# Modulation vectors of a two-block transformer step: sixteen of their pieces move from TensorE to VectorE, the others are gathered four to a bank

## The reference, cut to what matters

```python
c_act = jax.nn.silu(c)
for i in range(DEPTH):                          # DEPTH = 2
    mod = c_act @ w_mod[i] + b_mod[i]           # 1024 @ 1024 x 6144
    sh1, sc1, g1, sh2, sc2, g2 = jnp.split(mod, 6, axis=-1)
    h = modulate(rmsnorm(x, norm_mix[i]), sh1, sc1)     # h * (1 + sc1) + sh1
    y = pool_mixer(h, ...) if i == 0 else moba_attention(h, w_qkv, w_o, rel_bias)
    x = x + g1[:, None, :] * y
    h = modulate(rmsnorm(x, norm_mlp[i]), sh2, sc2)
    x = x + g2[:, None, :] * squared_relu_mlp(h, w_up[i], w_down[i])
return rmsnorm(x, norm_final)
```

## Time and profile before

| | us |
|---|---|
| median of 3 runs | 1115.1 (1113.09 to 1115.51) |
| the profiled execution's own time | 1114.1 |
| its span, first to last instruction | 1112.3 |
| TensorE busy | 1059.4 (95%) |
| VectorE busy | 771.5 (69%) |
| ScalarE busy | 534.8 (48%) |
| mean granted TensorE clock | 0.990 of full speed |

### The profile page before, as it was taken

One profiled execution on the slowest core, in us unless ns is written; L12 is line 12 of the kernel. 1 busy time (PEld: TensorE's weight loads), 2 busy tenths in 40 slices (PEclk: granted clock), 3 DMA queues, 4 the chain that ended last, 5 costly groups with the idle time before them and its releaser, 6 DMA issues.

```text
span 1112.3 us, 21636 instructions
## 1 busy us (share of the span) xinstructions
PE 1059.4 (95%) x8322; PEld 978.7 (88%) x8322; DVE 771.5 (69%) x1415; ACT 534.8 (48%) x862; POOL 1.7 (0%) x14
## 2 busy tenths in 40 slices
PE   5989999999999989999999999999989999999995
PEld 2469999999888868999999989989878999999995
DVE  5377767444556656877655589899897778777654
ACT  3345655433445545676544534538414565444341
POOL 0000000000000000000000000000000000000000
PEclk9999999999999999999999999999999999999998
DMA  9986666666646565455545435345443555555531
GB/s 360 369 336 252 249 245 229 242 247 226 210 174 218 180 242 227 156 185 189 189 174 204 151 114 200 141 152 209 136 147 119 222 190 183 181 182 183 205 126 38
DMA packets 35791, 222.10 MB, mean 200 GB/s; under 512 B 3804, under 2 KB 9101, under 8 KB 9357
## 3 DMA queue, kind: packets, MB, share of 16 engines
q1 hardware_dynamic: 35724, 221.18, 54.9%
HBM read 220.10 MB, written 1.07 MB: 199 GB/s over the span
## 4 chain that ended last, share of the span: by engine, by line
PE 83%; DVE 10%; ACT 3%; DMA 2%; issue 1%; SPq 0%; DVEq 0%; ACTq 0%
PE bank L534 23%; PE bank L535 22%; PE bank L536 22%; PE bank L785 6%; PE bank L556 4%; PE bank L835 3%; DVE y L1539 2%; PE bank L572 2%; DMA raw<-weights 2%; DVE w_lo L1230 1%; DVE rt L1602 1%; DVE newt L1236 0%; PE bank L705 0%; PE bank L579 0%; DMA x<-x_in 0%
## 5 line engine op out<-in xcount | busy, mean ns | idle before, releaser
L1230 DVE TENSOR_TENSOR w_lo<-raw,w_hi 128x1024 fp32r<-128x1024 f32 x270 | 327.8, 1218 | 65.4 <-ACT w_hi L896 64.3
L534 PE MATMUL bank<-xg_hi,w_hi 128*128 128x258 f32 (+1 forms) x1264 | 362.6, 287 | 5.8 <-DVE w_lo L1230 2.1
L535 PE MATMUL bank<-xg_lo,w_hi 128*128 128x258 f32 (+1 forms) x1264 | 357.9, 283 | 0.0
L536 PE MATMUL bank<-xg_hi,w_lo 128*128 128x258 f32 (+1 forms) x1264 | 357.6, 283 | 0.0
L896 ACT ACTIVATE w_hi<-raw 128x1024 fp32r<-128x1024 f32 x270 | 282.2, 1050 | 107.2 <-PE bank L536 91.1
L534 PEld LDWEIGHTS bank<-xg_hi,w_hi 128*128 128x128 f32 x1264 | 240.5, 190 | 14.0 <-issue 8.8
L535 PEld LDWEIGHTS bank<-xg_lo,w_hi 128*128 128x128 f32 x1264 | 240.0, 190 | 0.2
L536 PEld LDWEIGHTS bank<-xg_hi,w_lo 128*128 128x128 f32 x1264 | 239.8, 190 | 0.0
L534 PE MATMUL bank<-hid_hi,w_hi 128*128 128x256 f32 x512 | 144.7, 283 | 1.7 <-DVE ab L1359 1.7
L535 PE MATMUL bank<-hid_lo,w_hi 128*128 128x256 f32 x512 | 142.9, 279 | 0.0
L536 PE MATMUL bank<-hid_hi,w_lo 128*128 128x256 f32 x512 | 142.8, 279 | 0.0
(11 more groups left out here) (210 smaller groups left out, 1393.9 us busy)
## 6 DMA issues: line engine op xcount, KB each, us to landing
raw<-weights SPq DMA_DIRECT2D x157, 1024.0 KB, 4.8
mod_raw<-w_mod SPq DMA_DIRECT2D x48, 1024.0 KB, 6.2
toep<-bias_by_distance SPq DMA_DIRECT2D x8, 256.0 KB, 5.4
x<-x_in SPq DMA_DIRECT2D x1, 1024.0 KB, 5.0
toep<-bias_by_distance SPq DMA_DIRECT2D x8, 128.0 KB, 4.0
y_out<-yout SPq DMA_DIRECT2D x8, 128.0 KB, 1.8
invc<-inv_count SPq DMA_DIRECT2D x1, 512.0 KB, 13.0
vec<-vectors SPq DMA_DIRECT2D x1, 294.0 KB, 5.2
```

The lines of the kernel that those rows point to most:

```text
L534: pe.matmul(dst, hi, r_hi, start=start, stop=False, skip_group_check=True)
L535: pe.matmul(dst, hi, r_lo, start=False, stop=False, skip_group_check=True)
L536: return pe.matmul(dst, lo, r_hi, start=False, stop=stop, skip_group_check=True)
L1230: ve.tensor_tensor(w_lo[:, at % HL, :], raw[:, slot, (at % 2) * UT * P:(at % 2 + 1) * UT * P], w_hi[:, at % HL, :].bitcast(F32), ALU.subtr ...
```

## The change

The 48 pieces fall into two kinds, and the order in which they come is now a list, `PIECES`.

- **32 pieces stay on TensorE, in eight groups of four.** `cz` is 64 columns wide with the vector in column 31. `rows` of piece r of a group takes the columns from 31-r to 63-r, so that its result lands in row r of each column group, and all four pieces of a group accumulate in one bank. There is one `mod_copy` and one `cols` for a group; the moving operand of `cols` is `pick`, a 128x4 table that VectorE makes once from `ident`. Groups 0 to 4 are the twenty pieces before up0. Group 5 runs behind unit 12 of up0 and its `cols` behind unit 14; groups 6 and 7 run in qkv behind units 6 and 18, their `cols` behind units 10 and 22.
- **16 pieces go to VectorE.** They lie in memory with 128 features on the partitions and the 1024 inputs along the row. `dots` issues two `tensor_tensor_reduce` for each, 128x1024 float32, that multiply with `c_all` (the activated `c` on all partitions), add up, start from the bias, and write one column of `modv`. Twelve of them run in down0, at units 0, 1 and 4 of each eight, four in down1, at unit 0 of each eight.
- SyncE's queue loads all pieces into four slots, at places given by `PIECES_AFTER`. One more transfer spreads `c` over the partitions, and ScalarE applies Silu to it at unit 16 of up0.
- The gains of layer 1 are made from two features' chunks at a time in down0. `shift` for qkv is made at unit 30 instead of 24.
- Loops with a register as counter are written out in up0 and down0 and in half of up1 on all engines, and in down1 on VectorE. `cz` and `c_all` make the tiles larger by 5 KB per partition, and `pick` takes 16 bytes per partition ahead of `rstd`.

```diff
+ROWS = 4
+MOD_BASE = [8 * t for t in (SC1, SH1, G1, SC2, SH2)] + [48 + 8 * t for t in (G1, SC2, SH2)]
+MOD_AT = {("up0", 12): 5, ("qkv", 6): 6, ("qkv", 18): 7}
+COLS_AT = {("up0", 14): 5, ("qkv", 10): 6, ("qkv", 22): 7}
+DOTS = [(base, p) for p in range(4) for base in (8 * G2, 48 + 8 * SC1, 48 + 8 * SH1)] + [(48 + 8 * G2, p) for p in range(4)]
+DOTS_AT = {("down0", 8 * p + at): 3 * p + n for p in range(4) for n, at in enumerate((0, 1, 4))}
+DOTS_AT.update({("down1", 8 * p): 12 + p for p in range(4)})
+PIECES = [("rows", q) for q in range(24)] + [("dots", d) for d in range(12)] + [("rows", 24 + q) for q in range(8)]\
+    + [("dots", 12 + d) for d in range(4)]
+PIECES_AFTER = [2, 3, 4, 5, 13, 14, 15, 16, 23, 24, 25, 27, 28, 29, 31, 32, 33, 35, 36, 37, 41, 42, 43, 44, 48, 49, 50, 51]
...
             def piece(q, s):
 
-                if not isinstance(q, int) or q >= 4:
-                    sp.wait_ge(mod_rows, q - (3 if isinstance(q, int) and q < MOD_FIRST else 1))
-                sp.dma_start(mod_raw[:, s, :], w_mod[one(q)].rearrange("a p n -> p (a n)")).then_inc(mod_in[s], 16)
+                kind, n = PIECES[q]
+                if q >= 4:
+                    before, m = PIECES[q - 4]
+                    if before == "rows":
+                        sp.wait_ge(mod_rows, m + 1)
+                    else:
+                        sp.wait_ge(mod_dots, 2 * m + 2)
+                src = w_mod if kind == "rows" else w_dots
+                sp.dma_start(mod_raw[:, s, :], src[one(n)].rearrange("a p n -> p (a n)")).then_inc(mod_in[s], 16)
...
+            def pair_and_pieces(p):
+                pair(p, p % RAW)
+                if p == 6:
+                    sp.dma_start(c_all[:], bass.AP(c_row.tensor, 0, [[0, P], [1, D]])).then_inc(c_row_in, 16)
+                for q in pieces_after(p):
+                    piece(q, q % 4)
...
+            def rows(q):
+
+                g, r, n = q // ROWS, q % ROWS, ROWS_PIECE[q]
+                pe.wait_ge(mod_in[n % 4], 16 * (n // 4 + 1))
+                if r == 0 and g == 1:
+                    pe.wait_ge(var_done, 1)
+                if r == 0 and g >= 2:
+                    pe.wait_ge(mod_copied, g - 1 if q < MOD_FIRST else g)
+                row_bank = row_banks[g % 2 if q < MOD_FIRST else 0]
                 for k in range(DC):
-                    mm = pe.matmul(row_bank[32 * g:32 * g + 32, 0:SEQ], cz[:, k, :], mod_raw[:, s, SEQ * k:SEQ * (k + 1)],
-                                   start=k < 4, stop=k >= 4, tile_position=(0, 32 * g))
+                    c = k % 4
+                    mm = pe.matmul(row_bank[32 * c:32 * c + 32, 0:SEQ], cz[:, k, 31 - r:63 - r],
+                                   mod_raw[:, n % 4, SEQ * k:SEQ * (k + 1)], start=r == 0 and k < 4, stop=r == ROWS - 1 and k >= 4,
+                                   tile_position=(0, 32 * c), skip_group_check=True)
                 mm.then_inc(mod_rows, 1)
...
             for q in range(MOD_POOL):
-                rows(q, q % 4, mod_landed(q))
+                rows(q)
                 if q == 3:
                     pe.wait_ge(small_in, 48)
                     pe.matmul(banks[0][0:HEADS, 0:384], rbx[:], bkt[:], start=True, stop=True).then_inc(bias_mm, 1)
-                if q:
-                    cols(q - 1, (q - 1) % 2)
+                    pe.wait_ge(pick_done, 1)
+                if q % ROWS == 0 and q:
+                    cols(q // ROWS - 1)
...
+            def dots(d):
+
+                (base, p), n = DOTS[d], DOTS_PIECE[d]
+                if d == 0:
+                    ve.wait_ge(c_row_act, 1)
+                ve.wait_ge(mod_in[n % 4], 16 * (n // 4 + 1))
+                at = base + 2 * p
+                for half in range(2):
+                    w = mod_raw[:, n % 4, half * D:(half + 1) * D]
+                    ve.tensor_tensor_reduce(w, w, c_all[:], 1.0, col("b_mod", at + half), ALU.mult, ALU.add,
+                                            accum_out=modv[:, at + half:at + half + 1]).then_inc(mod_dots, 1)
+                ve.wait_ge(mod_dots, 2 * d + 2)
...
             def down(name, n, i, j, gate, gains):
+                mod_work(name, 8 * i + j)
                 if j % 4 < 3:
                     split(name, i, j)
```

More of the change, by code:

```diff
@@ L451, in _ @@
             for q in range(12, MOD_FIRST):
-                piece(q, mod_slot(q))
-            def mlp_loads(i):
-                for s in range(4):
-                    pair(4 * i + 1 + s, (1 + s) % RAW)
-                    if s >= 2:
-                        piece(2 * i + MOD_FIRST + s - 2, s - 2)
-            mlp_loads(0)
-            with sp.Fori(1, 8) as i:
-                mlp_loads(i)
+                piece(q, q % 4)
+            def pair_and_pieces(p):
[3 more added lines that the diff above has]
+                for q in pieces_after(p):
+                    piece(q, q % 4)
+            for p in range(1, U0["qkv"] // 2):
+                pair_and_pieces(p)
             def toeplitz(a):
@@ L484, in _ @@
                         toeplitz(a)
-                for q in range(DC):
-                    if n == max(1, (3 * q - 2) // 2 + 1):
-                        piece(36 + q, q % 2)
-            for a in range(4):
-                pair(p0 + 12 + a, (p0 + 12 + a) % RAW)
-                piece(44 + a, a % 2)
-            p0 += 16
+            for a in range(8):
+                pair_and_pieces(p0 + 12 + a)
+            p0 += 20
             loops = (U0["glu"] // 2 - p0) // RAW
@@ L571, in cols, with mod_work @@
                 for half in range(2):
-                    mm = pe.matmul(dst[:, at + half:at + half + 1], mod_row[:, s, half * P:(half + 1) * P],
-                                   ones[:, 0:1], start=True, stop=True)
+                    mm = pe.matmul(dst[:, ROWS * half:ROWS * half + ROWS], mod_row[:, g % 2, half * P:(half + 1) * P],
+                                   pick[:], start=True, stop=True)
                 mm.then_inc(mod_cols, 1)
+            def mod_work(name, v):
+                if (name, v) in MOD_AT:
+                    for r in range(ROWS):
+                        rows(ROWS * MOD_AT[name, v] + r)
+                if (name, v) in COLS_AT:
+                    cols(COLS_AT[name, v])
@@ L626, in whole @@
                 mm.then_inc(pe_units, 1)
-            def with_piece(i, j, base):
-                if j % 4 == 2:
-                    rows(2 * i + (MOD_FIRST + base + j // 4), j // 4, 16 * i + (landed_base(j // 4) + 16 + 16 * (base // 2)))
-                if j % 4 == 3:
-                    cols(2 * i + (MOD_FIRST + base + j // 4), j // 4)
-            def landed_base(s):
-                return 16 * sum(mod_slot(q) == s for q in range(MOD_FIRST))
             def down(name, i, j):
@@ L761, in _ @@
                             values(a)
-                        if j <= DC:
-                            cols(36 + j, j % 2)
+                        if j < DC:
+                            mod_work("qkv", v)
                         if j == DC:
@@ L924, in _ @@
             root(1)
-            for q in range(8):
-                mod_copy(q, q % 2)
+            for g in range(2):
+                mod_copy(g)
             act.wait_ge(xr_done, 1)
@@ L999, in down @@
                 if name == "down0":
-                    mod_piece(i, j, 8)
+                    mod_work(name, 8 * i + j)
                 split(name, i, j)
             up_phase("up0", 2)
-            act.wait_ge(gain_done, 3)
-            loop_units(act, "down0", lambda i, j: down("down0", i, j, 1, gain_at(2)))
+            for v in range(32):
+                down("down0", v // 8, v % 8, 1, gain_at(2))
             def exps(a, e):
@@ L1495, in _ @@
                     finish("o", 2, 0, j - 1, lambda m: gain[:, 3, one(m)])
-                if j % 2 == 1 and j < 6:
-                    mod_two(45 + j // 2)
             finish("o", 2, 0, 7, lambda m: gain[:, 3, one(m)])
             up_phase("up1", 4)
-            ve.wait_ge(mod_read, 33)
             clear(3, two=True)
-            loop_units(ve, "down1", lambda i, j: down("down1", 3, i, j, 48 + 8 * G2, lambda m: gain1[:, one(m)]))
+            for v in range(32):
+                down("down1", 3, v // 8, v % 8, 48 + 8 * G2, lambda m: gain1[:, one(m)])
             def scaled(name, v, w=SEQ):
```

230 lines of the change are left out of this document (112 added, 118 removed).

## The result

The changed kernel takes 1079.3 us, the median of four runs (1078.8 to 1081.1), against 1114.5 us for the kernel before on the same chip (four runs): a ratio of 0.969, interval 0.967 to 0.970. The forecast was 1081, in a range from 1072 to 1096. The profiled execution took 1079.2 us, of which 1077.3 are its span.

The account below looks back on a forecast made before the run. TensorE, busy for 95% of the span with 83% of the chain, was taken as the bound. 1114.1 - 5.5 (beginning) - 8.6 (up0) - 12.9 (down0) - 8.5 (qkv, o) + 2.0 (clock) = 1080.6; forecast 1081 us, range 1072 to 1096.

Parts of the forecast that it names:

- VectorE keeps ahead in down0: down0: VectorE's new instructions, 1.3 us each, stay hidden under TensorE's products up to 1.57 us each; 12.9 us gained.
- The first rival: down0: VectorE becomes the bound at 2.26 us per instruction, 14 us lost, 1095 us; chance 0.15.
- the prediction's 1.1: down0: at 1.3 us per instruction, the split for unit 12 of each eight is ready 1.1 us early.
- What a piece costs TensorE: From up0 on: one piece costs TensorE about 1.63 us, priced from stages that differ only in pieces.
- qkv and o: qkv and o: twelve pieces go, two groups come, 10.6 us; 8.5 us taken as arriving, bounds 5 and 10.6.
- a piece in the shadow of the slow transfers: qkv and o: one removed piece lies where TensorE idles behind late weight transfers, so 1.6 us is not gained.
- the last piece of group 7: qkv: this piece is loaded behind `toeplitz` and a pair, wanted some 9 us after; 0.5 us allowed as loss.
- The second rival: Beginning and attention: transfers and attention's own chain hold savings to 1 of 5.5 and 5 of 8.5 us; 1089 us; chance 0.13.
- The beginning: Before up0: `cols` of group 1 starts at 36 instead of 39.88 us; 5.5 us gained in all, bounds 1 and 8.
- The wait for `pick`: Beginning: TensorE's wait for this table, done by 23 us, is hidden by the transfers and costs nothing.
- The clock behind a group: Behind groups of four: the clock falls to half level after one of three groups, costing 2 us; bounds 0 and 6.
- The rest: Remaining stages: down1's new work is hidden, nothing gained or lost; 1 us left in the range for moved tiles.

Follow-up runs that it names:

- (3): The changed kernel with both VectorE reducing instructions of each of the 16 pieces on 8 instead of 1024 columns, transfers kept: 1078.9 us.
- (4): The changed kernel with one more 1024-column multiplication with sum on VectorE for each of down0's 12 pieces, result unused: 1086.0 us.
- (7): The changed kernel with the last two bias-table transfers, `toeplitz(6)` and `toeplitz(7)`, each issued one weight pair later in the queue: 1072.3 us.
- (6): The changed kernel with `cols` of groups 1 to 3 right behind its own group, not behind the next group's first `rows`: 1073.3 us.
- (8): Against the kernel before, gathering only: all 48 pieces stay on TensorE in twelve groups of four, none on VectorE: 1095.3 us, ratio 0.983.
- (11): The changed kernel with 24 tiny memsets added on VectorE before down1: 1077.1 us, a single execution.
- (10): The changed kernel with the edits of (6) and (7) together, and `pick` as spare columns of the `vec` tile: 1068.8 us.

## Why the prediction was right, step by step

**VectorE keeps ahead in down0: right.** The instruction takes 1.27 us and 0.08 for its sum, 1.3 forecast; the step between residuals is 11.31 us; and (3) shows that leaving out the arithmetic gives nothing. The first rival (2.26 us for each) is ruled out by the L1290 row. That the bound lay near is shown by (4): 6.3 us lost, where 14.7 us of the same work were added, because one split in each eight came 1.6 us late. The margin of that split in the changed kernel, 1.2 us, is the prediction's 1.1.

**What a piece costs TensorE: right.** down0 gave back 12.83 us, 12.9 forecast, and up0 8.73, 8.6 forecast. The price of 1.63 us came from twin stages, and it counts what busy time of the group doesn't.

**qkv and o: the mechanism right, the size too small.** 10.47 us came, 8.5 were forecast, 10.6 was the bound. TensorE's busy time fell by 146.02 - 134.92 = 11.1 us, which is 12 x 1.63 less two groups at 4.24. Idle time rose by 0.6. I had taken 1.6 us off for a piece in the shadow of the slow transfers and 0.5 for the last piece of group 7, 2.1 in all, and 0.1 came off the 10.6. The parts were not as I had them: the last piece of group 7 cost 1.60 us of waiting, not 0.5, while a wait of 1.66 us before a `cols` (at 301.5 us before) went with the single pieces. That the sum of idle time hardly changed is in part luck. The second rival named a real thing in the wrong form. The queue behind `toeplitz` is worth 7 us in the changed kernel; the change did not win them, and (7) does. The earlier trace rows show the same kind of wait in the kernel before, but no run took it away there.

**The beginning: the mechanism right, 0.9 us too much.** `cols` of group 1 came at 36.5 us, 36 forecast. The stretch from the pool stage to up0 gave 0.9 us where I had 1. Ahead of it 3.6 us came where I had counted 4.5: `cols` was half a microsecond later than I put it, and the copy inside the eight chunks of `h_pad` gave 0.3 us where 0.5 or so was counted. What I did not see is that the order of `cols` held back more than the change gave: (6) wins another 4.6 us up to up0 with one line moved. The wait for `pick` appears in the trace as 4.6 us of TensorE's time. Transfers keep running at 422 GB/s through it (20 to 24 us), and in (6), where the same wait is 4.7 us long, the chain goes past it along transfers. That speaks for a hidden wait, as forecast; no run took the wait away alone.

**The clock behind a group: wrong.** 2.0 us were counted and nothing came, in any of the three groups, nor in the seven of (8). The reasoning went from the beginning of the kernel before, where single `rows` and `cols` never brought the clock up, to a group at full speed. But four `rows` in a row are another thing: in the beginning of the changed kernel the clock rose within the first group, at 16 us. The three times that it fell in qkv and o it stood at or behind waits of 1.6 to 2.0 us: before at 304 and 410 us, after at 371. Waits of that length do not always bring it down (1.60 us at 350 us in the changed kernel, 2.36 us inside a group of (8)).

**The rest: 1.7 us not foreseen.** The last down stage went over to the slower pace (+2.34), the stage before it to the quicker (-1.10), and 0.49 us came between down1 and that earlier stage (288.07 to 288.56 us), where no run tells why; over all kernels here this stretch takes between 288.07 and 289.86 us. This is luck of the program and no part of the prediction.

The terms make 1080.6 - 2.0 (clock) - 2.0 (qkv) + 0.9 (beginning) + 1.7 (rest) = 1079.2 us, the time of the profiled execution. The errors were each of 1 to 2 us and took one another away, so the forecast's 2 us are better than its parts.

## What to carry to other kernels

Price small work on the engine that bounds the kernel from two stages that differ only in it; here that gave 1.63 us, where busy time showed 1.37 for each piece's 16 `rows`, and the stages then shrank by that price within 0.2 us. Work a ceiling per instruction out of the order in time, not only out of the sum, before an engine is given work under another's cover, and test it with more of the same work: what fits by the sum, or nearly, can lack its place in the order. And look at what each result stands behind: a product that waits for the next piece's transfer, or weights queued behind a table that waits for attention, cost 6 and 7 us here, a third of what the whole change gave.

## What the runs showed of the hardware that was not expected

The multiplication with a running sum over two float32 tiles, 128x1024, takes 1.27 us, 0.05 more than a plain subtraction, with a separate 0.08 us instruction to read the sum; two of each together take 2.53 us.

The same list of products, at a granted clock of 1.00, runs at 0.113 or at 0.117 us each, in the last down stage and, with (11), in down1. In the one program that was traced twice it came out the same. It changes the length of a stage by up to 3 us when instructions elsewhere, on another engine even, are added. A difference of 2 to 3 us between two versions of this kernel can come from this alone, so the stage in which it arises has to be looked up before it is put down to an edit.

After some waits of TensorE of 1.0 to 2.0 us the clock stood at the half level for 3.4 or 6.8 us at a time (304 and 410 us before, 371 after, 367 and 384 in (10)), and after others of 1.3 to 2.4 us it did not. It did not fall behind 3.7 us of `rows` at full speed, and within the first four `rows` in a row, at 16 us, it rose. Where VectorE sets the pace, near 795 us, twice as long at the half level cost nothing that the traces show.
